# Hybrid state-space, attention and mixture-of-experts layer: forget gates in four column groups of TensorE, two sets of transposes on VectorE, and another order of attention's first steps

## The reference, cut to what matters

```python
h = rmsnorm(x, norm_mix_g); q, k, v, f_logit, u = split(h @ w_in)       # 512 | 512 | 512 | 8 | 512 columns
log_f = log_sigmoid(f_logit + b_f)                                       # forget gates, 8 heads
attn  = forgetting_attention(q, k, v, log_f)                             # scores + cumsum(log_f)[t] - cumsum(log_f)[s], causal
g     = gelu(s5_scan(u) + d_skip * u); ssm = g * sigmoid(g @ w_glu + b_glu)
x     = x + concat(rmsnorm(attn), rmsnorm(ssm)) @ w_out
h     = rmsnorm(x)                                                       # 1024 rows of 1024
logits = h @ w_router + b_router                                         # 32 experts, top 4, softmax of the 4
x     = x + moe(h); x = x + sigmoid(rmsnorm(x) @ w_ple_gate) * (p @ w_ple_proj); out = rmsnorm(x)
```

## Time and profile before

| | |
|---|---|
| median of 3 timed runs | 2353.3 us (2353.11 to 2354.07) |
| the profiled execution's own time | 2335.39 us |
| its span, first to last instruction | 2334.0 us |
| TensorE / VectorE / ScalarE / GpSimd busy | 98% / 40% / 18% / 26% of the span |
| mean granted TensorE clock | 0.994 of full speed |
| DMA | 528.05 MB, mean 226 GB/s |

### The profile page before, as it was taken

One profiled execution on the slowest core, in us unless ns is written; L12 is line 12 of the kernel. 1 busy time (PEld: TensorE's weight loads), 2 busy tenths in 40 slices (PEclk: granted clock), 3 DMA queues, 4 the chain that ended last, 5 costly groups with the idle time before them and its releaser, 6 DMA issues.

```text
span 2334.0 us, 40365 instructions
## 1 busy us (share of the span) xinstructions
PE 2277.5 (98%) x15218; PEld 1588.5 (68%) x15218; DVE 936.0 (40%) x2090; ACT 429.1 (18%) x877; POOL 603.5 (26%) x915
## 2 busy tenths in 40 slices
PE   8999999999799999999999999999999999999998
PEld 5545566555455577878878788778887888767443
DVE  4644467233644343433434434323333222212474
ACT  3110166411411111111101111011111000000344
POOL 0546588100222312122121121222212111111320
PEclk9999999999899999999999999999999999999999
DMA  5100010300499999899898899878887666542540
GB/s 195 41 24 6 24 53 4 156 36 28 172 406 401 399 411 363 322 322 330 315 329 318 321 325 333 289 279 313 320 313 283 252 245 239 202 168 101 208 168 36
DMA packets 98716, 528.05 MB, mean 226 GB/s; under 512 B 21863, under 2 KB 22551, under 8 KB 46559
## 3 DMA queue, kind: packets, MB, share of 16 engines
q1 hardware_dynamic: 72383, 460.19, 52.8%
q0 software_dynamic: 26272, 67.02, 8.3%
HBM read 494.74 MB, written 31.23 MB: 225 GB/s over the span
## 4 chain that ended last, share of the span: by engine, by line
PE 85%; DMA 6%; DVE 4%; ACT 3%; issue 1%; SPq 1%; POOL 0%; POOLq 0%; ACTq 0%; DVEq 0%
PE ps L1847 38%; PE ps L1860 16%; DMA wg<-in_w_gu 5%; PE ps L1608 5%; PE ps L1896 3%; PE ps L1599 2%; PE ps L1721 2%; PE ps L1726 2%; PE ps L1874 2%; DVE x L1459 2%; PE ps L1627 1%; PE ps L1661 1%; PE ps L1701 1%; PE ps L1977 1%; PE ps L1865 1%
## 5 line engine op out<-in xcount | busy, mean ns | idle before, releaser
L1847 PEld LDWEIGHTS ps<-xT,wg 128*128 128x128 f32 x6912 | 873.0, 191 | 26.6 <-issue 13.5
L1847 PE MATMUL ps<-xT,wg 128*128 128x128 f32 (+3 forms) x6912 | 889.1, 291 | 0.0
L1446 DVE TENSOR_SCALAR gb<-ps,bcur 128x256 f32<-128x256 f32 x216 | 104.5, 484 | 830.5 <-PE ps L1847 830.5
L1860 PE MATMUL ps<-wd,actT 128*128 128x512 f32 x864 | 375.6, 592 | 0.0
L1860 PEld LDWEIGHTS ps<-wd,actT 128*128 128x128 f32 x864 | 162.5, 190 | 193.8 <-issue 187.3
L890 ACT ACTIVATE sg<-gb 128x256 f32<-128x256 f32 x216 | 90.0, 417 | 785.9 <-DVE gb L1446 785.9
L580 POOL DMA_INDIRECT xg<-normalised_rows,rowc x184 | 177.9, 967 | 74.1 <-issue 45.1
L611 POOL COPY rowc<-rowq 128x8 uint32 (+1 forms) x34 | 6.3, 187 | 570.3 <-DVE xT L1399 570.3
L1896 PE MATMUL ps<-wg,xT 128*32 128x256 f32 x2304 | 134.5, 386 | 10.0 <-DVE xT L1399 6.4
L629 POOL DMA_DIRECT2D bin__179<-in_b_exp x33 | 18.9, 574 | 415.2 <-issue 288.0
L1977 PE MATMUL ps<-wpg,xnT 128*128 128x512 f32 x256 | 112.9, 595 | 5.9 <-ACT xnT L902 5.9
(11 more groups left out here) (405 smaller groups left out, 2363.0 us busy)
## 6 DMA issues: line engine op xcount, KB each, us to landing
wg<-in_w_gu SPq DMA_DIRECT2D x264, 1024.0 KB, 7.0
wd<-in_w_dn SPq DMA_DIRECT2D x132, 1024.0 KB, 6.8
expert_rows<-yb POOLq DMA_DIRECT2D x48, 256.0 KB, 8.5
expert_rows<-yb POOLq DMA_DIRECT2D x60, 128.0 KB, 4.5
hT<-in_x_cm SPq DMA_DIRECT2D x8, 512.0 KB, 8.6
cumb<-gate_sums SPq DMA_DIRECT2D x4, 1024.0 KB, 4.7
x<-in_x_tm SPq DMA_DIRECT2D x1, 4096.0 KB, 13.4
wout<-in_w_out SPq DMA_DIRECT2D x1, 4096.0 KB, 20.9
```

Source lines behind the costliest of these rows:

```text
L1446: v.tensor_scalar(gb[:, f % 2, :], ps[:, f % 2, 0:W], bcur[:, f:f + 1], 7.0, ALU.add, ALU.min).then_inc(S("g_ready"), 1)
L1847: ins = m.matmul(ps[:, f % 2, g_ * W:g_ * W + w], wg[:, f, k, g_, :], xT[:, k, 0:w], start=(k == 0), stop=(k == KT - 1))
L1860: ins = m.matmul(ps[:, 2 + c, :], actT[:, f, 0:P], wd[:, c, f, :], start=(f == 0), stop=(f == FT - 1))
```

## The change

- The forget gates' eight matmuls per block go to four column groups of the array (output partitions 0, 32, 64 and 96, two matmuls in each). VectorE copies one group's result and adds the other three before it scales.
- `gtm` is laid out in quarters; SyncE moves it with 16 DMAs from SBUF to SBUF into `gx`, partitions regrouped, and VectorE turns `gx` into `gT` with four stream transposes during the last three tiles of attention. The 32 TensorE transposes and the eight ScalarE copies go. The rows of `w_glu`, `b_glu`, the gain and `w_out` are reordered on the host to match.
- For router blocks 0 to 5 SyncE, after it has stored a block, loads it back in four DMAs with quarters of rows in quarters of the partitions (`hq`), and VectorE turns it with one stream transpose between the two halves of `resid`; a second copy of the router's weights, `wrq`, has its rows in the matching order. Blocks 6 and 7 keep TensorE's transposes; block 6's move ahead of project(7, 1).
- On VectorE row_low(3) comes before recip(1) and recip(2). A wait for the gains' load ahead of the GLU's products goes.
- Some semaphores are merged.

```diff
@@ SyncE @@
+            sp.wait_ge(S("gel_out"), 8)
+            for r in range(4):
+                for a_ in range(4):
+                    sp.dma_start(gx[32 * a_:32 * a_ + 32, r, :, :], gtm[32 * r:32 * r + 32, a_, :, :]).then_inc(S("gx_ld"), 16)
             sp.wait_ge(S("tr_mm"), 2 * UNITS[NT])
...
-            sp.wait_ge(S("gt_mm"), 8)
             sp.dma_start(wr[:, :, :], w_router).then_inc(S("out_ld"), 16)
+            sp.wait_ge(S("gl_mm"), 8)
+            sp.dma_start(wrq[:, :, :], w_router_q).then_inc(S("aux_ld"), 16)
             for t in range(8):
                 sp.wait_ge(S("hn_ready"), t + 1)
                 sp.dma_start(hs[...], hn[:, t, :]).then_inc(S("hs_st"), 16)
+                if t < 6:
+                    sp.wait_ge(S("hs_st"), 16 * t + 16)
+                    if t >= 2:
+                        sp.wait_ge(S("ht_evac"), t - 1)
+                    for a_ in range(ND):
+                        sp.dma_start(hq[32 * a_:32 * a_ + 32, t % 2, :].rearrange("j (r d) -> j r d", r=4), quarter_rows(t, a_)).then_inc(S(f"quart_ld{t % 2}"), 16)
@@ VectorE @@
-                    link(v.tensor_tensor(zh, ps[0:8, bank, :], rbr[0:8, 512 * un[1]:512 * un[1] + 512], ALU.mult))
+                    link(v.tensor_copy(zh, ps[0:8, bank, :]))
+                    for j in range(1, 4):
+                        link(v.tensor_tensor(zh, ps[32 * j:32 * j + 8, bank, :], zh, ALU.add))
+                    link(v.tensor_tensor(zh, zh, rbr[0:8, 512 * un[1]:512 * un[1] + 512], ALU.mult))
...
             recip(0)
+            row_low(AHEAD)
             recip(1)
             for s in range(NT):
                 if s + 2 < NT:
                     recip(s + 2)
-                if s + AHEAD < NT:
+                if s and s + AHEAD < NT:
...
+                if s >= NT - AHEAD:
+                    if s == NT - AHEAD:
+                        dve.wait_ge(S("gx_ld"), 256)
+                    for r in ((0, 1), (2,), (3,))[s - NT + AHEAD]:
+                        v.transpose(gT[:, :, :].rearrange("p c (t r j) -> p r t c j", r=4, j=32)[:, r],
+                                    gx[:, r, :, :].rearrange("p t (c i) -> p t c i", i=32)).then_inc(S("gt_evac"), 1)
             heads_out(NT - 1)
-            dve.wait_ge(S("glu_ld"), 32)
...
+            def router_turn(t):
+                dve.wait_ge(S(f"quart_ld{t % 2}"), 64 * (t // 2) + 64)
+                if t >= 2:
+                    dve.wait_ge(S("rt_mm"), t - 1)
+                turn_32(v, h2T[:, t % 2, :, :], hq[:, t % 2, :]).then_inc(S("ht_evac"), 1)
             for t in range(8):
                 resid(t, 0)
+                if 1 <= t < 7:
+                    router_turn(t - 1)
                 resid(t, 1)
                 norm_rows(t)
@@ TensorE @@
                     for k in range(KT):
-                        ins = m.matmul(ps[0:8, bank, :], wf[:, k, :], hT[...], start=(k == 0), stop=(k == KT - 1))
+                        j = 32 * (k % 4)
+                        ins = m.matmul(ps[j:j + 8, bank, :], wf[:, k, :], hT[...], start=(k < 4), stop=(k >= 4))
...
-            for t in range(8):
-                if t >= 4:
-                    pe.wait_ge(S("gt_evac"), t - 3)
-                for c in range(4):
-                    ins = m.transpose(ps[:, t % 4, c * P:c * P + P], gtm[:, t, 8 * c:8 * c + 8, :].rearrange("p g c -> p (g c)"), ident)
-                ins.then_inc(S("gt_mm"), 1)
-            pe.wait_ge(S("gt_evac"), 8)
+            pe.wait_ge(S("gt_evac"), 4)
...
-            turn_rows(0)
             for t in range(1, 7):
                 project(t + 1, 0)
                 route(t - 1)
+                if t == 6:
+                    turn_rows(6)
                 project(t + 1, 1)
-                turn_rows(t)
```

More of the change, by code:

```diff
@@ L106, in build @@
 def build(nc, x_cm, x_tm, pT, small, consts, b_f, d_skipT, b_router, gains, w_in, w_glu, w_out,
-          w_router, w_gu, w_dn, b_exp, b_gu, b_dn, w_ple_gate, w_ple_proj, out, hs, ys, cum):
+          w_router, w_router_q, w_gu, w_dn, b_exp, b_gu, b_dn, w_ple_gate, w_ple_proj, out, hs, ys, cum):
     with ExitStack() as ctx:
@@ L244, in build @@
         h2T = at("h2T", [P, 2, KT, P], F32, R_K)
-        selq = at("selq", [P, 4, ND, 32], F32, R_K + 8192)
+        selq = at("selq", [P, 4, ND, 32], F32, R_S)
+        hq = at("hq", [P, 2, D], F32, R_K + 8192)
+        wrq = at("wrq", [P, KT, 32], F32, R_S + 4096)
         wr = at("wr", [P, KT, 32], F32, R_U)
@@ L320, in scores_of, with quarter_rows, turn_32 @@
             return sc01[:, s % 2] if s % 4 < 2 else sc23[:, s % 2]
+        def quarter_rows(t, a_):
+            return hs[ND * P * t:ND * P * t + ND * P, :].rearrange("(r j a) d -> a j r d", r=4, a=ND)[a_]
+        def turn_32(v, dst, src):
+            return v.transpose(dst.rearrange("p c (r j) -> p r c j", r=4), src.rearrange("p (r c i) -> p r c i", r=4, i=32))
         block = ctx.enter_context(nc.Block())
@@ L326, in _ @@
         def _(sp):
-            sp.dma_start(par[:, 0:O_GSSM], small[:, 0:O_GSSM]).then_inc(S("gain_ld"), 16)
+            sp.dma_start(par[:, 0:O_GSSM], small[:, 0:O_GSSM]).then_inc(S("aux_ld"), 16)
             for k in range(KT):
@@ L1601, in _ @@
                     for k in range(KT):
-                        ins = m.matmul(ps[0:8, bank, :], wf[:, k, :], hT[:, k, 512 * un[1]:512 * un[1] + 512], start=(k == 0), stop=(k == KT - 1))
+                        j = 32 * (k % 4)
+                        ins = m.matmul(ps[j:j + 8, bank, :], wf[:, k, :], hT[:, k, 512 * un[1]:512 * un[1] + 512], start=(k < 4), stop=(k >= 4))
                 else:
@@ L1736, in turn_rows @@
                 pe.wait_ge(S("wo_evac"), 3)
-                if t:
-                    pe.wait_ge(S("ht_evac"), t)
+                if t == 7:
+                    pe.wait_ge(S("ht_evac"), 7)
                 for k in range(KT):
@@ L1749, in route @@
                     at_, lo = (96 - 32 * k, 0) if k < 3 else (0, 32 * (k - 3))
-                    ins = m.matmul(ps[:, 6 + t % 2, at_:at_ + P], h2T[:, t % 2, k, :], wr[:, :, :].rearrange("p k e -> p (k e)")[:, lo:lo + P],
+                    ins = m.matmul(ps[:, 6 + t % 2, at_:at_ + P], h2T[:, t % 2, k, :], (wr if t >= 6 else wrq)[:, :, :].rearrange("p k e -> p (k e)")[:, lo:lo + P],
                                    start=(k == 0), stop=(k == KT - 1), skip_group_check=True)
@@ L1764, in _ @@
             pe.wait_ge(S("sm_ready"), 1)
-            turn_rows(0)
+            pe.wait_ge(S("aux_ld"), 32)
             for t in range(1, 7):
@@ L2017, in kmaj, with quarters, quarters_512 @@
         return cont(a.reshape(-1, P, a.shape[-1]).transpose(1, 0, 2))
+    def quarters(a):
+        a = A(a)
+        return cont(a.reshape(ND, KT, 32, a.shape[-1]).transpose(0, 2, 1, 3).reshape(P, KT, a.shape[-1]))
+    def quarters_512(a):
+        a = A(a)
+        return cont(a.reshape((4, 4, 32) + a.shape[1:]).swapaxes(1, 2).reshape((P, 4) + a.shape[1:]))
     def pairs(a):
```

46 lines of the change are left out of this document (22 added, 24 removed).

## The result

The changed kernel takes 2333.84 us (median of 4 runs, 2333.03 to 2337.06), the kernel before 2353.20 us on the same chip (4 runs, 2351.51 to 2354.07): ratio 0.9922, 95% interval 0.9908 to 0.9936, 19.4 us less. The forecast was 2332.6 us, 20.7 us less. Measured twice more against new runs of the kernel before, the ratio is 0.9926 (0.9909 to 0.9942) and 0.9925 (0.9911 to 0.9938): 17.5 and 17.4 us less. So the size is 17 to 19 us. The profiled execution after has an own time of 2333.47 us and a span of 2331.9 us.

The account below looks back on a forecast made before the run. TensorE, 85% of the chain of waits, was taken to bound the kernel. Gains of 10.2 + 3.0 + 3.1 + 4.4 = 20.7 us brought the timed median from 2353.3 to 2332.6 us, range 2327 to 2341 us.

Parts of the forecast that it names:

- Part 1: Forget gates: four column groups cut TensorE's time from 13.9 to 3.7 us; gain 10.2 us, at most 10.4.
- Rival (b): Forget gates: column groups give nothing for 8-column matmuls; 10.5 us less in all, 2342.8 us; chance 0.05.
- Part 2: Attention's first steps: gap 2.2 instead of 2.94 us, clock staying up; gain 3.0 us, bounds 0.5 and 3.6.
- rival (a): Attention's start: the clock falls all the same; 18.7 us less in all, 2334.6 us; chance 0.25.
- slightly the likelier: Attention's start: the clock staying up was favoured, the gap being a quarter shorter with work on both sides.
- Part 3: State-space turn by DMAs and VectorE: 4.7 us of transposes and copies go, less delays; gain 3.1 us.
- the last values end at 419.1 (1.4 us late): Attention's end: VectorE's stream transposes delay the last tiles' copies, so the values end 1.4 us later.
- Part 4: Router: six of eight blocks lose 0.87 us of TensorE transposes each; gain 4.4 us, bounds 0 and 5.2.
- (c): Router's loop: the store, load and transpose ring binds, loads taking 4 us more than counted; 2339 us; chance 0.08.
- (d): Router's loop: the round trip takes 16 us where 8 were counted, making the kernel slower; chance 0.03.
- Net (6 - 1) x 0.87 = 4.4 us: Router: six blocks' transposes saved, less block 6's, which move out of a wait where they hid; 4.4 us.
- Its parts are those of the timed runs: Whole kernel: the profiled 2335.4 us execution has the same parts as timed runs of median 2353.3 us.

Follow-up runs that it names:

- order_only: The kernel before with only row_low(3) moved ahead of recip(1) and recip(2): 2351.20 us, ratio 0.9995.
- after_no_router: The changed kernel with all eight router blocks turned by TensorE and copied by ScalarE again: 2318.81 us, ratio 0.9927.
- after_no_order: The changed kernel with attention's first steps in the old order on VectorE: 2318.33 us, ratio 0.9925.
- before_again: The kernel before, unedited, measured and traced a second time: 2352.75 us, ratio 1.0002.
- tail_filled: The changed kernel with gelu's first halves behind odd tiles, block 6's transposes behind the last projection, identity transposes in TensorE's router-end waits: 2328.15 us, ratio 0.9894.
- after_turn6_late: The changed kernel with only block 6's TensorE transposes put back behind the last projection: 2332.77 us, ratio 0.9912.
- both_edits: The changed kernel with GpSimd's first halves of gelu behind odd tiles and block 6's transposes back behind the last projection: 2313.43 us, ratio 0.9903.
- after_again: The changed kernel, unedited, measured and traced again: 2318.26 us, 17.5 us under the kernel before.

## Why the prediction was right, and where it was not

**Part 1, right.** 3.55 us against 3.7 us from the experts' row, so a gain of 10.3 us against 10.2, and 10.8 by the run with this part alone. Four column groups of 8 columns each are worth 13.83 / 3.55 = 3.9 times; the figure of 2.38x for three groups in the Trainium skill (TensorE: Matmul & The Clock Gate, part 3), scaled as the prediction did, would give an estimated 4.4 us, and the trace disagrees with it. Rival (b) falls. That VectorE's side costs nothing held too.

**Part 2, right by the traces and open in the timed runs.** The five traces with the old order, all with a fall, take 20.4 us to the values on average (19.19 to 20.98). With the new order and the clock up it is 17.4 us: 3.0 us, the forecast term. That is an average: against the very trace that the forecast was made from it is 20.98 - 17.40 = 3.6 us, the upper bound, since from the transposes to the values it took 293.79 - 289.11 = 4.68 us where 5.62 us were counted. With the new order and a fall (order_only, after_no_router) it is 18.8 us, on average a gain of 1.6 where rival (a) said 1.0; but the kernel before alone spreads by 1.8 us here (19.19 and 20.98), by how long its fall lasts, so that price is not settled. Of six traces with the gap of 2.44 us the clock held in four, so "slightly the likelier" was fair. But after_no_order is no slower than the changed kernel by medians, so in timed runs the 3.0 us do not all show.

**Part 3, mis-sized low.** Forecast 3.1 us; measured 4.1 us up to the GLU in the traces, 4.6 us in the timed runs with this part alone. The mis-sized term is "the last values end at 419.1 (1.4 us late)": they came 4.7 - 4.1 = 0.6 us late by it, not 1.4, and the fourth transpose ended at 404.80, before the values at 404.86, not behind them. A further 0.1 to 0.5 us is the wait for the gains, which the prediction had at nothing: the profile's chain of the first trace did not pass through it, that of before_again did.

**Part 4, right in the loop and wrong at its end.** The loop is as forecast: 15.5 us a turn, no idle, slack in the ring, so rivals (c) and (d) fall. The step that failed is "Net (6 - 1) x 0.87 = 4.4 us": it counts transposes at full clock and puts the clock of what follows at nothing. In all seven traces with the new router and nothing filled in, the last router matmuls run mostly at 1.2 GHz and take 3.42 to 3.78 us; in all six with the old router they run at 2.4 GHz and take 2.05 us. In the changed kernel that is 1.4 us, so 4.4 became 3.2 us on the span. With block 6's transposes back in the wait and the clock held (tail_filled) the span is 140.85 - 135.60 = 5.2 us shorter, which is the 6 x 0.87 us of the prediction's upper bound.

Block 6's move also emptied the wait that its transposes had filled, and TensorE idles 3.03 us there in place of 0.93. But that idle is not what brings the fall: after_turn6_late and both_edits have 0.93 us again, and their router matmuls still take 3.63 and 3.58 us. Why the new router loses the clock there and the old one does not, although both end in the same instructions, stays open; what tail_filled shows is that work in the waits holds it. In the timed runs this part is worth 0.55 us (after_no_router), and putting block 6 back where it was wins 3.0 us, more than any trace shows. The prediction asked for the clock at attention's start and not here, where the same question stood.

The stretch from the last routing to the experts is 40.5 us on average in the three traces of the changed kernel and 39.7 us in the six with the old router. That is not shown to be the change's doing: after_no_order, with the new router, has 38.8 us. The stretch moves with when a fall of the clock begins in it (the first eight residual matmuls take 3.70 us in the first trace of before, 4.28 us in order_only, 4.81 us in after_no_router) and with how long the experts' first rows take to come (2.85 us in the chain of the first trace of before, 3.51 us in that of after).

**The sum.** 10.3 + 3.0 + 4.1 + 0.3 + 3.2 = 20.9 us from the traces up to the last routing, against 20.7 forecast; with the 0.8 us lost behind it 20.1 us. The first trace of before and after_again's, both of the lower level, differ by 2335.39 - 2315.29 = 20.1 us. That the total comes so near is in part luck: part 3 was 1.0 us too low, part 4 1.2 us too high, and the 0.3 us of the gains' wait and what lies behind the router were not in the sum. The timed medians give 17.4 to 19.4 us. Most timed runs of the changed kernel have a mean clock of 0.992 to 0.994 and its traces 0.995, so the 1 to 3 us between may well be clock; in those runs themselves it was not seen.

**Two slips in its working**, which move nothing in the forecast. In rival (d) 2358 us belongs to the round trip of 16 us; at 17 us its own terms give 5 x 7.7 - 7 - 20.7 = 10.8 us slower, 2364 us. The lower bound of part 3 is 3.1 - 2.4 = 0.7 us by its own terms, not 0.5.

**"Its parts are those of the timed runs", wrong.** The 18 us between the profiled execution and the median were the two levels, not one kernel's spread. It cost the forecast nothing, since the change does not touch the experts.

## What to carry to other kernels

When a change touches TensorE's stream ahead of a stretch of short waits, ask for the clock of the matmuls in that stretch too: here its fall took 1.4 of the forecast 4.4 us. And when work is moved out of a wait, test the move by itself in timed runs: putting eight transposes back won 3.0 us there, of which the trace shows 0.5. Where short waits follow each other, a few matmuls that nobody reads, sized from the waits' own rows and ended before the release, can be worth more than the last microsecond of rearranging: 3.2 us here by the traces. Compare a trace only with timed runs of the same chip and session, stage by stage from fixed starts: 17 us here belonged to one of these and not to the kernel.

## What the runs showed that was not expected

- The clock's fall is not set by one idle. Gaps of 2.44 us kept it in four traces and lost it in two; idles of 0.93 and 1.11 us in the same place kept it in after_no_router and lost it in both_edits. Filling the waits held it in the trace of tail_filled, and all four of its runs have a mean clock of 0.997. The Trainium skill (TensorE: Matmul & The Clock Gate, part 1) says that the default state is throttled and activity releases it; tail_filled agrees, 2.05 against 3.58 us for the same matmuls.
- Chips or sessions differ. With the same code, a group of the experts' second product took 64.6 us on one chip and 73.8 to 74.9 us on others, the difference in waits for issue, none for data. What it is that issues more slowly there was not tried.
- A fall of the clock at attention's start lasts about 3 us in one execution and about 7 us in another of the same kernel behind the same gap of 2.94 us (before_again, where the granted clock is 0.50 from 298 to 301, 0.80 in 301 to 302 and 1.00 in 302 to 303; and 299 to 306 in the earlier trace rows).
- A stream transpose of 128 x 1024 elements out of rows just brought by DMA costs what it does elsewhere: 1.20 to 1.22 us for `gT` and 1.23 to 1.25 us for `h2T`, against 1.22 us.
